# Where the first products' weights of a merge stage are loaded and split: in the merge itself, or during the stage before it

## The chip, the cores and the metric
One Trainium2 chip, the kernel on one core of it. The metric is the device time of one execution in microseconds (us), lower is better. TensorE is called PE, VectorE DVE, ScalarE ACT, GpSimd POOL; SyncE (SP) issues nearly all transfers.

## The reference, cut to what matters
One decoder layer on 2048 prompt rows and on 8 sequences of 4 new rows with 512 cached keys each. Two attention branches (differential attention a, forgetting attention b) share a projected input and are merged. The part that matters here:

```python
def _merge(x, o_a, o_b, gate_a, gate_b, m_a, m_b, gate_res, g_sub_a, w_out_a, w_out_b, w_o, lam_init):
    o_a = _rms(o_a) * g_sub_a * (1.0 - lam_init)
    y_a = (o_a.reshape(B, T, W_A) * jax.nn.silu(gate_a)) @ w_out_a
    y_b = (o_b.reshape(B, T, W_B) * jax.nn.silu(gate_b)) @ w_out_b
    y = (jax.nn.sigmoid(m_a) * y_a + jax.nn.sigmoid(m_b) * y_b) @ w_o
    return x + gate_res[:, None, :] * y
```

`w_out_a` and `w_out_b` are 512x1024, `w_o` is 1024x1024, all float32. The sample branch before it (`_sample_mix`) gathers each sequence's cached K and V pages, computes scores, softmax and the products with V. Everything is to be computed at about float32 precision.

## The kernel before
The program is a row of blocks with a barrier between them: normalise and project (two halves), maxima, attention a, attention b, **sample** (the 8 sequences' attention over the cache) and **merge** (17 tiles: 16 of 128 prompt rows, one of the 32 sample rows). Each block has one instruction stream per engine, written out by hand with semaphores; the order in the code is the order on the engine.

**Split products.** For near-float32 precision a product is made of three matmuls in a rounded format: each operand is kept as a high part (rounded) and a low part (operand less high part). `split_product` (L454) issues high x high, high x low, low x high. Weights are thus first loaded raw, then ACT copies them into the high part (L2234 in the merge), then DVE subtracts to get the low part (L2324).

**sample.** K and V pages of a sequence b (4 MB) go into one of two buffer sets by b's parity `s`; SP loads K(b) when K(b-2) has been turned and V(b) when the products with V(b-2) are done. Each turn of the loop `body(i, s)` with b = 2i+s does, besides work on sequence b, the K part of b+1: PE turns K(b+1) in eight pieces, DVE (L1900) and ACT (L1974) copy them out of PSUM, PE computes the scores of b+1, DVE adds biases and takes the maximum (L1923 to L1928), ACT the exponentials (L1984), PE multiplies probabilities of b by V. Then DVE scales and masks the result (`own_columns`, L1935) and adds it up (L1940). At the end `o_sum` is stored for the merge.

**merge.** One tile's turn: ACT squares o_a and takes sigmoids of gates (`square`, L2203, L2205) and mix (`mixing`, L2209); DVE makes u (`gated`, L2262 to L2275); PE transposes u, ACT and DVE split it (uT, L2224, L2281); PE forms both first products into ps_y (`products`, weights `w_out_a`, `w_out_b`); DVE combines them (`combine`, L2290 to L2293) into y; PE transposes y, ACT and DVE split it; PE multiplies by `w_o` into ps_o (`project_out`); DVE finishes (L2300, L2302) and SP stores. Tile n+1's u is made while tile n's products run. The first turn is written out apart, because the weights are loaded and split in it: 16 tiles of 128x1024 (kt 0 to 3 of `w_out_a`, 4 to 7 of `w_out_b`, 8 to 15 of `w_o`), through four raw buffers of which two are `x` and `out`, `w_split` counting DVE's subtractions. SP may load tile kt when `w_split` is kt-3. PE waits for `w_split` 4 and 8 before the first products and for 16 before the loop over the other tiles; SP waits for 16 before it loads x and the rows of tile 2.

Of the kernel before, what the change touches and what calls it, by code (L numbers as in the profile page):

```python
# [24 lines left out]
P = 128  # L25
# [15 lines left out]
W = 512  # L41
# [37 lines left out]
def program(nc, t):  # L79
    with ExitStack() as ctx:  # L80
# [22 lines left out]
        sample(k)  # L103
        merge(k)
# [1609 lines left out]

def sample(k):
# [10 lines left out]
    with ExitStack() as ctx:  # L1726
# [15 lines left out]
        ones = sb("ones", [NB * HB, PAST])  # L1742
        f_past = sb("f_past", [NB * HB, PAST])
# [15 lines left out]
        o_sum = sb("o_sum", [SR, 2, W])  # L1759
# [12 lines left out]
        with nc.Block() as block:  # L1772
            @block.sync
            def _(sp):
# [15 lines left out]
                def next_v(b, s):  # L1790
                    sp.wait_ge(S["made"], 1)
                    sp.wait_ge(S["pv_done"], b - 1)
                    load(b, s, 1)

                for what in range(2):
                    load(0, 0, what)
                    load(1, 1, what)
                next_k(2, 0)
                with sp.Fori(1, TURNS - 1) as i:
                    next_k(i * 2 + 1, 1)  # L1800
                    next_v(i * 2, 0)
                    next_k(i * 2 + 2, 0)
                    next_v(i * 2 + 1, 1)
                next_k(NB - 1, 1)
                next_v(NB - 2, 0)
                next_v(NB - 1, 1)
# [6 lines left out]
            def _(pool):  # L1813
# [10 lines left out]
                g.memset(ones[:], 1.0)  # L1824
# [35 lines left out]
            def _(dve):  # L1860
# [43 lines left out]
                go(v.tensor_tensor_scan(f_past[:], ones[:], ps_f, 0.0, ALU.mult, ALU.add))  # L1904
                v.tensor_scalar(f_rel[:], f_past[:], f_past[:, PAST - 1:PAST], None, ALU.subtract).then_inc(S["f_ready"], 1)
                dve.wait_ge(S["fn_ready"], 1)
                v.tensor_copy(f_new[:], ps_n[0:HB, 0:SR]).then_inc(S["fn_copied"], 1)
                go(v.memset(o_sum[:], 0.0))
# [29 lines left out]
                def add(b):  # L1938
                    dve.wait_ge(S["picked"], b + 1)
                    v.tensor_tensor(o_sum[:], ps_o[0:SR, :, :], o_sum[:], ALU.add).then_inc(S["added"], 1)  # L1940
# [4 lines left out]
                def body(i, s, first, last):  # L1945
# [14 lines left out]
                    if not last:  # L1960
                        biased(b + 1)

# [5 lines left out]
            def _(act):  # L1968
# [114 lines left out]
def merge(k):  # L2083
# [4 lines left out]
    KT = 2 * KW + KD  # L2088
    weights = [t["w_out_a"][0]] * KW + [t["w_out_b"][0]] * KW + [t["w_o"][0]] * KD
    w_row = [kt % KW if kt < 2 * KW else kt - 2 * KW for kt in range(KT)]  # L2090
    x_in = {P: t["x_prompt"][0], SR: t["x_sample"].rearrange("b t d -> (b t) d")}
    with ExitStack() as ctx:
        sb, ps, sem = tools(k, ctx, "mrg")
        w_raw = sb("w_raw", [P, 2, D])
        w = [sb("w_hi", [P, KT, D], F32R), sb("w_lo", [P, KT, D], F32R)]
# [29 lines left out]
        with nc.Block() as block:  # L2125
            @block.sync
            def _(sp):
# [20 lines left out]
                for kt in range(KT):  # L2148
                    if kt >= NW:
                        sp.wait_ge(S["w_split"], kt - NW + 1)  # L2150
                    r = w_row[kt] * P
                    sp.dma_start(w_slots[kt % NW], weights[kt][r:r + P, :]).then_inc(w_in[kt % NW], 16)
# [43 lines left out]
            def _(act):  # L2196
# [40 lines left out]
                w_high(range(2 * KW))  # L2237
                square(1, P)
                mixing(0, P)
# [194 lines left out]
```

## Time and profile before

| | us |
|---|---|
| median of 3 runs | 3129.6 (3125.41, 3134.66, 3129.6) |
| profiled execution | 3128.66 |
| its span, first to last instruction | 3127.1 |
| sample stage, first K load issued to its last store issued | 2405.68 to 2660.46 |
| merge, first transfer issued to the end | 2662.67 to 3127.1 |

The mean granted TensorE clock over the span is 0.94 of full speed. A time in the trace is counted in us from the start of the span. "Idle" is the time in which an engine had nothing before an instruction, with the instruction of another engine or the transfer that ended it.

### The profile page before, as it was taken

How to read it: one execution, taken by the hardware profiler on the slowest of the kernel's cores; microseconds unless marked ns; L12 is line 12 of the kernel's file. 1: busy time of each engine (PE TensorE's matmuls, PEld its weight loads, DVE VectorE, ACT ScalarE, POOL GpSimd, SP SyncE). 2: the span in 40 equal slices, each digit the busy share in tenths (PEclk: the TensorE clock that was granted, in tenths of full speed). 3: DMA queues.
4: the chain of work that ended last, by engine and by line, in shares of the span. 5: the costliest groups of instructions: out<-in, count | busy, mean ns of one | idle time of the engine just before them, and what ended most of it. 6: DMA issues, size and time to landing. Idle time of an engine off the chain costs nothing. (4 is left out here: it accounts for less than half of the span.)

```text
span 3127.1 us, 36974 instructions
## 1 busy us (share of the span) xinstructions
PE 2787.6 (89%) x12679; PEld 2050.4 (66%) x12679; DVE 1656.6 (53%) x2864; ACT 1040.2 (33%) x1742; POOL 196.7 (6%) x177
## 2 busy tenths in 40 slices
PE   5699999967999789999996999699997888499999
PEld 1488888855777566767774776477775322388886
DVE  2422135634265466667772776588887222545553
ACT  0411112233122256660002777555554111322221
POOL 1000002220022220000000000000001000000000
PEclk9799999987999889999997999899999899699999
DMA  5332355434453364433327562535352441533431
GB/s 209 116 101 77 101 189 156 130 123 125 148 157 104 104 134 114 117 98 95 91 76 166 133 138 62 104 82 118 74 112 77 161 149 54 202 133 124 131 127 56
DMA packets 277142, 372.85 MB, mean 119 GB/s; under 512 B 78515, under 2 KB 169779, under 8 KB 269205
## 3 DMA queue, kind: packets, MB, share of 16 engines
q1 hardware_dynamic: 275898, 370.67, 42.1%
q8 instruction: 73, 1.20, 0.2%
q14 instruction: 73, 0.60, 0.1%
q0 software_dynamic: 1056, 0.13, 0.1%
q10 hardware_dynamic: 42, 0.25, 0.0%
HBM read 259.90 MB, written 111.07 MB: 119 GB/s over the span
## 5 line engine op out<-in xcount | busy, mean ns | idle before, releaser
L454 PE MATMUL proj_z<-proj_w_hi,h_hi 128*128 128x512 f32 (+1 forms) x1200 | 475.3, 396 | 0.0
L454 PE MATMUL proj_z<-proj_w_hi,h_lo 128*128 128x512 f32 (+1 forms) x1200 | 469.8, 391 | 0.0
L454 PE MATMUL proj_z<-proj_w_lo,h_hi 128*128 128x512 f32 (+1 forms) x1200 | 468.7, 391 | 0.0
L1213 DVE TENSOR_REDUCE max_neg_top<-max_s_ps 128x1 f32<-128x1024 f32 (+7 forms) x384 | 347.1, 911 | 137.9 <-PE max_s_ps L1278 91.1
L454 PEld LDWEIGHTS proj_z<-proj_w_hi,h_lo 128*128 128x128 f32 (+1 forms) x1200 | 221.4, 185 | 53.5
L454 PEld LDWEIGHTS proj_z<-proj_w_lo,h_hi 128*128 128x128 f32 (+1 forms) x1200 | 221.9, 185 | 50.1
L454 PEld LDWEIGHTS proj_z<-proj_w_hi,h_hi 128*128 128x128 f32 (+1 forms) x1200 | 221.6, 185 | 49.7
L1624 ACT ACTIVATE att_b_pf<-att_b_s_ps,att_b_bias 128x512 f32<-128x512 f32 (+1 forms) x320 | 193.4, 624 | 160.2 <-PE att_b_s_ps L1675 80.4
L1652 DVE TENSOR_TENSOR att_b_p_lo<-att_b_pf,att_b_p_hi 128x512 fp32r<-128x512 f32 (+1 forms) x320 | 195.9, 612 | 11.0
L1177 ACT ACTIVATE max_s_ps<-max_s_ps,max_neg_top 128x128 f32<-128x128 f32 (+2 forms) x192 | 161.0, 838 | 107.0 <-DVE max_neg_top L1213 106.2
L1302 PE MATMUL max_z<-gate_w_hi,h_lo 128*128 128x512 f32 (+1 forms) x432 | 178.8, 414 | 0.0
L1302 PE MATMUL max_z<-gate_w_hi,h_hi 128*128 128x512 f32 (+1 forms) x432 | 177.9, 412 | 0.0
L1302 PE MATMUL max_z<-gate_w_lo,h_hi 128*128 128x512 f32 (+1 forms) x432 | 177.6, 411 | 0.0
L1407 ACT ACTIVATE att_a_pf<-att_a_s_ps,att_a_bias 128x1024 f32<-128x1024 f32 (+3 forms) x160 | 158.1, 988 | 53.1 <-PE att_a_s_ps L1480 32.4
L581 POOL TENSOR_TENSOR proj_rstd<-proj_rstd,keep_neg_half 128x8 f32<-128x8 f32 (+1 forms) x68 | 111.5, 1639 | 833.7 <-DVE proj_rstd L755 833.7
L1273 PE MATMUL max_s_ps<-map_k,map_q 128*128 128x512 f32 (+2 forms) x320 | 124.8, 390 | 38.4 <-ACT max_s_ps L1177 23.0
L701 DVE CAST proj_w_hi<-proj_w_raw 128x512 fp32r<-128x512 f32 x144 | 60.6, 421 | 183.9 <-PE proj_z L454 175.3
L1650 DVE CAST att_b_p_hi<-att_b_pf 128x512 fp32r<-128x512 f32 (+1 forms) x320 | 121.8, 381 | 65.6 <-ACT att_b_pf L1624 58.5
L1424 DVE SCALAR_TENSOR_TENSOR att_a_pc<-att_a_pf,keep_neg_lam 128x512 f32<-128x512 f32 (+3 forms) x160 | 106.9, 668 | 86.5 <-ACT att_a_pf L1407 86.2
L1674 PE MATMUL att_b_s_ps<-att_b_q,att_b_k 128*128 128x512 f32 (+1 forms) x320 | 121.3, 379 | 26.0 <-DMA att_b_bias<-scratch_bias_col 26.0
L683 ACT ACTIVATE proj_z_sb<-proj_z 128x512 f32<-128x512 f32 (+1 forms) x68 | 40.6, 597 | 305.7 <-PE proj_z L454 305.7
L1707 PE MATMUL att_b_acc<-att_b_p_hi,att_b_v 128*128 128x512 f32 (+1 forms) x320 | 129.6, 405 | 9.5 <-DVE att_b_p_lo L1652 9.5
(326 smaller groups left out, 5317.6 us busy)
## 6 DMA issues: line engine op xcount, KB each, us to landing
proj_w_raw<-in_w_in SPq DMA_DIRECT2D x144, 256.0 KB, 3.5
mrg_mix<-scratch_mixes SPq DMA_DIRECT2D x16, 1024.0 KB, 4.8
ada_w<-in_w_ada SPq DMA_DIRECT2D x8, 1536.0 KB, 9.1
map_qm<-scratch_q_hi SPq DMA_DIRECT2D x48, 256.0 KB
gate_w_raw<-in_w_in SPq DMA_DIRECT2D x44, 256.0 KB, 4.1
map_k<-scratch_k_hi SPq DMA_DIRECT2D x37, 256.0 KB
norm_x_in<-in_x_prompt SPq DMA_DIRECT2D x4, 2048.0 KB, 10.3
scratch_mixes<-proj_out SPq DMA_DIRECT2D x32, 256.0 KB, 2.2
```

Source lines behind the costliest of these rows:

```text
L454: ins = nc.tensor.matmul(out, left(*lt), right(*rt), start=first and n == 0, stop=last and n == len(terms) - 1)
L581: nc.gpsimd.tensor_tensor(rstd[0:pn, :], rstd[0:pn, :], k.neg_half[0:pn, :], ALU.pow).then_inc(rstd_done, 1)
L1177: nc.scalar.activation(s, s, ACT.Exp, bias=neg_top[:, kh, u, qt:qt + 1], accum_out=sums[:, kh, u, qt:qt + 1]).then_inc(sum_done, 1)
L1213: nc.vector.tensor_reduce(neg_top[:, kh, u, qt:qt + 1], s_ps[:, x % SLOTS, 0:width[x]], AX.X, ALU.max, negate=True).then_inc(max_done, 1)
L1273: nc.tensor.matmul(o, q2, k2, start=True, stop=False)
L1302: last = nc.tensor.matmul(z[0:rows_of(j), n % 2, :], h_parts[hp][:, kt, rows_j], gw.parts[wp][:, c % 2, kt, :], start=m == 0, stop=m == MM ...
L1407: nc.scalar.activation(pf[:, n % PR, :, 0:w], s_ps[:, n % PLACES, :, 0:w], ACT.Exp, bias=a.bias[h % 2][:, col:col + 1]).then_inc(p_done, 1)
L1624: nc.scalar.activation(pf[:, n % PR, 0:w], s_ps[:, n % 4, 0:w], ACT.Exp, bias=bias[s][:, kt:kt + 1]).then_inc(p_done, 1)
L1650: step.inc(nc.vector.tensor_copy(parts[HI][:, n % PR, 0:w], pf[:, n % PR, 0:w]))
L1652: nc.vector.tensor_tensor(parts[LO][:, n % PR, 0:w], pf[:, n % PR, 0:w], parts[HI][:, n % PR, 0:w].bitcast(F32), ALU.subtract).then_inc(sp ...
L1674: nc.tensor.matmul(out, k2[s][:, ks], q2[s][:, qs], start=True, stop=False)
L1707: nc.tensor.matmul(out, v[s][:, kt, 0:P], p_hi, start=kt == 0, stop=False, skip_group_check=True)
```

## The change
A new object `out_weights` holds the high and low parts of `w_out_a` and `w_out_b` and a raw buffer of two tiles, allocated around both sample and merge. In the sample stage each turn now also loads one 128x1024 tile (slot 0 from `w_out_a`, slot 1 from `w_out_b`, i the tile's number), rounds it on ACT and subtracts on DVE. The merge splits only the eight tiles of `w_o`. Its orders are rewritten for that: SP issues the first mix load ahead of weights and tile 1's rows behind the fourth weight tile, ACT does `mixing(0)` ahead of the weights, and DVE does four subtractions, `gated(1)`, two, `combine(0)`, low part, two. PE's two waits ahead of the first products go. To make room, `ones`, `f_past` and `o_sum` of the sample stage share one buffer `scan`; the memset of `o_sum` waits for `f_rel`.

```diff
+def load_out_w(k, sp, i, s):
+    w = k.out_w
+    sp.dma_start(w.raw[:, s:s + 1, :], w.src[s][:, ds(i, 1), :]).then_inc(w.loaded[s], 16)
+def out_w_high(k, act, i, s):
+    act.wait_ge(w.loaded[s], i * 16 + 16)
+    k.nc.scalar.activation(w.parts[HI][:, s:s + 1, ds(i, 1), :], w.raw[:, s:s + 1, :].unsqueeze(2), ACT.Copy).then_inc(w.hi_done[s], 1)
+def out_w_low(k, dve, i, s):
+    dve.wait_ge(w.hi_done[s], i + 1)
+    k.nc.vector.tensor_tensor(w.parts[LO][:, s:s + 1, ds(i, 1), :], w.raw[:, s:s + 1, :].unsqueeze(2),
+                              w.parts[HI][:, s:s + 1, ds(i, 1), :].bitcast(F32), ALU.subtract).then_inc(w.lo_done[s], 1)
...
+                def next_v(b, s, i):
                     sp.wait_ge(S["made"], 1)
                     sp.wait_ge(S["pv_done"], b - 1)
                     load(b, s, 1)
+                    sp.wait_ge(k.out_w.lo_done[s], i)
+                    load_out_w(k, sp, i, s)
                 for what in range(2):
                     load(0, 0, what)
                     load(1, 1, what)
+                for s in range(2):
+                    load_out_w(k, sp, 0, s)
                 next_k(2, 0)
...
                     if not last:
                         biased(b + 1)
+                    out_w_low(k, dve, i, s)
...
                     if not last:
                         k_turned(b + 1)
                         probabilities(b + 1)
+                    out_w_high(k, act, i, s)
...
                 load_o(0, P)
-                for kt in range(KT):
+                load_m(0, P)
+                for kt in range(KD):
                     if kt >= NW:
                         sp.wait_ge(S["w_split"], kt - NW + 1)
...
-                    if kt == 2 * KW - 1:
-                        load_m(0, P)
+                    if kt == NW - 1:
                         sp.wait_ge(S["u_done"], 1)
                         load_o(1, P)
-                sp.wait_ge(S["w_split"], KT)
+                sp.wait_ge(S["w_split"], KD)
                 load_x(0, P)
...
-                w_low(range(2 * KW))
+                w_low(range(4))
                 gated(1, P)
-                w_low(range(2 * KW, KT - 4))
+                w_low(range(4, KD - 2))
                 combine(0, P, True)
                 low(1, P, S["uT_hi_done"], uT, S["uT_done"])
-                w_low(range(KT - 4, KT))
+                w_low(range(KD - 2, KD))
                 low(0, P, S["yT_hi_done"], yT, S["yT_done"])
...
                     for b in range(2):
-                        if first:
-                            pe.wait_ge(S["w_split"], (b + 1) * KW)
```

On SP, at the merge's start, before (`mrg_ob`, `mrg_gates`: a tile's attention rows and gates; `mrg_w_raw`, `mrg_x`, `mrg_out`: the four raw weight buffers):

```order
L2130 DMA mrg_ob<-scratch_o_a 128x512
L2130 DMA mrg_ob<-scratch_o_b 128x512
L2131 DMA mrg_gates<-scratch_gates 128x1024
L2152 DMA mrg_w_raw<-in_w_out_a 128x1024 x2
L2152 DMA mrg_x<-in_w_out_a 128x1024
L2152 DMA mrg_out<-in_w_out_a 128x1024
L2152 DMA mrg_w_raw<-in_w_out_b 128x1024 x2
L2152 DMA mrg_x<-in_w_out_b 128x1024
L2152 DMA mrg_out<-in_w_out_b 128x1024
L2134 DMA mrg_mix<-scratch_mixes 128x2048
L2130 DMA mrg_ob<-scratch_o_a 128x512
L2130 DMA mrg_ob<-scratch_o_b 128x512
```

and after the change (`wo_raw`: the new raw buffer, now the first two of the four):

```order
L2167 DMA mrg_ob<-scratch_o_a 128x512
L2167 DMA mrg_ob<-scratch_o_b 128x512
L2168 DMA mrg_gates<-scratch_gates 128x1024
L2171 DMA mrg_mix<-scratch_mixes 128x2048
L2189 DMA wo_raw<-in_w_o 128x1024 x2
L2189 DMA mrg_x<-in_w_o 128x1024
L2189 DMA mrg_out<-in_w_o 128x1024
L2167 DMA mrg_ob<-scratch_o_a 128x512
L2167 DMA mrg_ob<-scratch_o_b 128x512
L2168 DMA mrg_gates<-scratch_gates 128x1024
L2189 DMA wo_raw<-in_w_o 128x1024 x2
L2189 DMA mrg_x<-in_w_o 128x1024
```

The eight loads of `w_out_a` and `w_out_b` are gone from here, mix stands ahead of the weights, and tile 1's rows stand behind four weight loads and not behind eight.

On DVE, from the low part of tile 0's uT to the reduction of tile 1, before:

```order
L2281 TENSOR_TENSOR mrg_uT_lo<-mrg_ps_t,mrg_uT_hi 128x512 x2
L2324 TENSOR_TENSOR mrg_w_lo<-mrg_w_raw,mrg_w_hi 128x1024 x2
L2324 TENSOR_TENSOR mrg_w_lo<-mrg_x,mrg_w_hi 128x1024
L2324 TENSOR_TENSOR mrg_w_lo<-mrg_out,mrg_w_hi 128x1024
L2324 TENSOR_TENSOR mrg_w_lo<-mrg_w_raw,mrg_w_hi 128x1024 x2
L2324 TENSOR_TENSOR mrg_w_lo<-mrg_x,mrg_w_hi 128x1024
L2324 TENSOR_TENSOR mrg_w_lo<-mrg_out,mrg_w_hi 128x1024
L2262 TENSOR_REDUCE mrg_ms<-mrg_u 128x4
```

and after, up to the combination of tile 0:

```order
L2317 TENSOR_TENSOR mrg_uT_lo<-mrg_ps_t,mrg_uT_hi 128x512 x2
L2360 TENSOR_TENSOR mrg_w_lo<-wo_raw,mrg_w_hi 128x1024 x2
L2360 TENSOR_TENSOR mrg_w_lo<-mrg_x,mrg_w_hi 128x1024
L2360 TENSOR_TENSOR mrg_w_lo<-mrg_out,mrg_w_hi 128x1024
L2298 TENSOR_REDUCE mrg_ms<-mrg_u 128x4
L2300 TENSOR_SCALAR mrg_ms<-mrg_ms 128x4
L2302 TENSOR_TENSOR mrg_gates<-mrg_gates,mrg_y 128x1024
L2304 TENSOR_TENSOR mrg_gates<-mrg_gates,mrg_gain 128x512
L2306 TENSOR_TENSOR mrg_u<-mrg_ob,mrg_gates 128x512
L2311 SCALAR_TENSOR_TENSOR mrg_u<-mrg_ob,mrg_rstd,mrg_gates 128x128 x4
L2360 TENSOR_TENSOR mrg_w_lo<-wo_raw,mrg_w_hi 128x1024 x2
L2326 TENSOR_TENSOR mrg_y<-mrg_ps_y,mrg_mix 128x1024
```

Four of the subtractions ahead of tile 1's gating are gone, and two of the four between gating and combination.

On ACT, in the sample stage, the end of a loop turn before (`smp_pr`: the exponentials):

```order
L1977 REGISTER_ALU
L1978 ACTIVATE smp_sc<-smp_ps_s 32x512
L1982 ISA
L1984 ACTIVATE smp_pr,smp_sums<-smp_sc,smp_neg_max 32x544 x2
L1853 REGISTER_ALU
L1853 COMPARE_AND_BRANCH
```

and after:

```order
L2016 REGISTER_ALU
L2017 ACTIVATE smp_sc<-smp_ps_s 32x512
L2021 ISA
L2023 ACTIVATE smp_pr,smp_sums<-smp_sc,smp_neg_max 32x544 x2
L1738 ISA
L1738 ACTIVATE wo_hi<-wo_raw 128x1024
L1890 REGISTER_ALU
L1890 COMPARE_AND_BRANCH
```

The copy into the weights' high part stands behind the exponentials, ahead of the next turn's K copies.

## Rows read from the trace of the kernel before

**Rows 1.** The page, parts 1 and 4: busy time; chain by engine.
```profile
PE 2787.6 (89%) x12679; PEld 2050.4 (66%) x12679; DVE 1656.6 (53%) x2864; ACT 1040.2 (33%) x1742; POOL 196.7 (6%) x177
...
PE 12%; DVE 1%; DMA 1%; ACT 0%; issue 0%; SPq 0%; DVEq 0%; ACTq 0%
```

**Rows 2.** Chain of waits in order, merge: start us, us, what.
```profile
2663.56 4.88 DMA mrg_ob<-scratch_o_b
...
2678.27 1.29 DVE mrg_uT_lo L2281 x2
2679.56 4.55 DVE mrg_w_lo L2324 x4
...
2686.18 8.69 DMA mrg_gates<-scratch_gates
...
2704.13 1.13 DVE mrg_y L2290
...
2707.65 1.20 DVE mrg_uT_lo L2281 x2
2708.85 3.23 DVE mrg_w_lo L2324 x3
...
2713.41 0.33 SPq L2138
...
2715.70 8.83 DMA mrg_mix<-scratch_mixes
...
2733.59 12.96 PE mrg_ps_o L454 x48
...
2747.42 11.21 PE mrg_ps_y L454 x48
```

**Rows 3.** Timeline of the merge's start: start us, us, engine, line, operation, [idle <-releaser].
```profile
2678.12 2.00 ACT L2234 ACTIVATE mrg_w_hi<-mrg_w_raw 128x1024 fp32r<-128x1024 f32 x2
...
2684.24 0.76 PE L454 MATMUL mrg_ps_y<-mrg_w_hi,mrg_uT_hi 128*128 128x512 f32 x1 [7.13 <-DVE mrg_w_lo L2324]
...
2694.26 0.69 DVE L2262 TENSOR_REDUCE mrg_ms<-mrg_u 128x4 f32<-128x512 f32 x1 [2.17 <-ACT mrg_u L2203]
...
2694.89 1.06 ACT L2205 ACTIVATE mrg_y<-mrg_gates 128x1024 f32<-128x1024 f32 x1 [0.66 <-DMA mrg_gates<-scratch_gates]
...
2695.85 1.91 ACT L2209 ACTIVATE mrg_mix<-mrg_mix 128x2048 f32<-128x2048 f32 x1
2695.98 1.23 DVE L2266 TENSOR_TENSOR mrg_gates<-mrg_gates,mrg_y 128x1024 f32<-128x1024 f32 x1 [0.83 <-ACT mrg_y L2205]
...
2697.70 0.39 PE L454 MATMUL mrg_ps_y<-mrg_w_hi,mrg_uT_lo 128*128 128x512 f32 x1
...
2699.51 2.35 DVE L2324 TENSOR_TENSOR mrg_w_lo<-mrg_w_raw,mrg_w_hi 128x1024 fp32r<-128x1024 f32 x2
...
2731.62 1.97 PE L2349 MATMUL mrg_ps_t<-keep_ident,mrg_u 128*128 128x128 f32 x8 [5.03 <-DVE mrg_u L2275]
```

**Rows 4.** Timeline of the sample stage: ACT and DVE, first turn and end.
```profile
2461.48 0.18 ACT L1984 ACTIVATION_READ_ACCUMULATOR smp_pr<-smp_sc,smp_neg_max 32x1 f32 x1
...
2466.83 1.40 DVE L1935 SCALAR_TENSOR_TENSOR smp_o_own<-smp_ps_o,smp_recip,smp_own 32x512 f32<-32x512 f32 x2 [6.86 <-PE smp_ps_o L2075]
2467.85 0.60 ACT L1974 ACTIVATE smp_kT<-smp_ps_t 128x512 f32<-128x512 f32 x1 [6.19 <-PE smp_ps_t L2013]
...
2655.43 1.40 DVE L1935 SCALAR_TENSOR_TENSOR smp_o_own<-smp_ps_o,smp_recip,smp_own 32x512 f32<-32x512 f32 x2 [11.47 <-PE smp_ps_o L2075]
```

**Rows 5.** Windows: start:end, length, busy PE, PEld, DVE, ACT, POOL; clock; DMA share, GB/s.
```profile
2440.00:2445.00 5.00, 4.29 (x20) 3.40 (x20) 1.38 (x2) 2.59 (x7) 0.00 (x0) 0.54 0.00 0
...
2668.00:2672.00 4.00, 0.00 (x0) 0.00 (x0) 1.36 (x3) 2.97 (x3) 1.04 (x1) 0.50 1.01 415
...
2684.00:2688.00 4.00, 3.76 (x9) 3.02 (x10) 1.32 (x2) 1.88 (x2) 0.00 (x0) 0.50 0.99 300
2688.00:2692.00 4.00, 4.00 (x15) 3.16 (x15) 3.58 (x3) 2.35 (x3) 0.00 (x0) 0.80 1.01 417
```

More of the change, by code:

```diff
@@ L102, in program @@
         recycle(k)
-        sample(k)
-        merge(k)
+        with ExitStack() as c4:
+            out_weights(k, c4)
+            sample(k)
+            merge(k)
 def tools(k, ctx, tag):
@@ L1712, in _, with out_weights @@
                     turn(N - 1)
+def out_weights(k, ctx):
+    nc, t = k.nc, k.t
+    _, _, sem = tools(k, ctx, "wo")
+    w = Store()
+    w.parts = [ctx.enter_context(nc.sbuf_tensor(f"wo_{n}", [P, 2, W // P, D], F32R, side="right")) for n in ("hi", "lo")]
+    w.raw = ctx.enter_context(nc.sbuf_tensor("wo_raw", [P, 2, D], F32, side="right"))
+    w.src = [t[n][0].rearrange("(a p) n -> p a n", p=P) for n in ("w_out_a", "w_out_b")]
+    w.loaded, w.hi_done, w.lo_done = [sem("loaded0"), sem("loaded1")], [sem("hi0"), sem("hi1")], [sem("lo0"), sem("lo1")]
+    k.out_w = w
+def load_out_w(k, sp, i, s):
+    w = k.out_w
+    sp.dma_start(w.raw[:, s:s + 1, :], w.src[s][:, ds(i, 1), :]).then_inc(w.loaded[s], 16)
+def out_w_high(k, act, i, s):
+    w = k.out_w
+    act.wait_ge(w.loaded[s], i * 16 + 16)
+    k.nc.scalar.activation(w.parts[HI][:, s:s + 1, ds(i, 1), :], w.raw[:, s:s + 1, :].unsqueeze(2), ACT.Copy).then_inc(w.hi_done[s], 1)
+def out_w_low(k, dve, i, s):
+    w = k.out_w
+    dve.wait_ge(w.hi_done[s], i + 1)
+    k.nc.vector.tensor_tensor(w.parts[LO][:, s:s + 1, ds(i, 1), :], w.raw[:, s:s + 1, :].unsqueeze(2),
+                              w.parts[HI][:, s:s + 1, ds(i, 1), :].bitcast(F32), ALU.subtract).then_inc(w.lo_done[s], 1)
 def sample(k):
@@ L1741, in sample @@
         tri = sb("tri", [SR, SR])
-        ones = sb("ones", [NB * HB, PAST])
-        f_past = sb("f_past", [NB * HB, PAST])
+        scan = sb("scan", [NB * HB, 2, PAST])
+        ones, f_past = scan[:, 0, :], scan[:, 1, :]
         f_rel = sb("f_rel", [NB * HB, PAST])
@@ L1758, in sample @@
         o_own = sb("o_own", [ROWS, 2, W])
-        o_sum = sb("o_sum", [SR, 2, W])
+        o_sum = scan[0:SR]
         ps_t = ps("ps_t", [P, 2, 512])
@@ L1823, in _ @@
                 g.memset(tri[:], 1.0)
-                g.memset(ones[:], 1.0)
+                g.memset(ones, 1.0)
                 g.memset(q_all[:], 0.0).then_inc(S["filled"], 1)
@@ L1903, in _ @@
                 dve.wait_ge(S["lf_turned"], 1)
-                go(v.tensor_tensor_scan(f_past[:], ones[:], ps_f, 0.0, ALU.mult, ALU.add))
-                v.tensor_scalar(f_rel[:], f_past[:], f_past[:, PAST - 1:PAST], None, ALU.subtract).then_inc(S["f_ready"], 1)
+                go(v.tensor_tensor_scan(f_past, ones, ps_f, 0.0, ALU.mult, ALU.add))
+                v.tensor_scalar(f_rel[:], f_past, f_past[:, PAST - 1:PAST], None, ALU.subtract).then_inc(S["f_ready"], 1)
                 dve.wait_ge(S["fn_ready"], 1)
                 v.tensor_copy(f_new[:], ps_n[0:HB, 0:SR]).then_inc(S["fn_copied"], 1)
-                go(v.memset(o_sum[:], 0.0))
+                dve.wait_ge(S["f_ready"], 1)
+                go(v.memset(o_sum, 0.0))
                 dve.wait_ge(S["consts"], 1)
@@ L2243, in _ @@
                 evacuate(1, P, uT[HI], S["uT_hi_done"])
-                w_high(range(KT - 4, KT))
+                w_high(range(KD - 2, KD))
                 act.wait_ge(S["y_turned"], 1)
```

33 lines of the change are left out of this document (14 added, 19 removed).

## The prediction
> **What bounds the kernel now.** First the page, its parts 1 and 4 [rows 1]. TensorE is busy 89% of the span, and the chain that ended last is 12% PE with 1% each of DVE and DMA. This chain begins with the merge's first transfer, so it says what a microsecond is worth in the merge and nothing of the sample stage; that one is read from idle times below. Second, the chain in order of time [rows 2]. From 2733.59 on it is TensorE alone, 11.21 us for 48 matmuls, turn after turn. Between 2663.56 and 2733.59 it is a start-up of 70 us in which PE is late nearly everywhere: the first attention rows (4.88), the low part of the first uT (1.29), four subtractions for the weights' low halves (4.55), the second tile's transfers (8.69), more subtractions, combine and the low part of the second tile, again four subtractions (2708.85 to 2713.41), then SP's loads for tile 2 (mix lands 8.83 us after its issue). Everything after 2733.59 only shifts with that point. So the change is worth what it takes out between 2663.56 and 2733.59, less what it adds to the sample stage.
>
> **What the change takes out of the merge.** Before, 16 weight tiles are rounded on ACT and subtracted on DVE in the merge; after, eight. I follow the chain with the durations of the trace.
> 1. Up to the low part of uT ACT and DVE have the same instructions as before. It ends at 2679.56 [rows 2].
> 2. First products. Before, they wait until DVE has subtracted four tiles: first matmul at 2684.24, with 7.13 us of idle time put down to that subtraction [rows 3]. After, both parts of these weights exist, so they start at about 2679.7. They take what they took, from 2684.24 to the last start at 2697.70 plus some 0.4: 13.85 us, of which a part is slow (the first matmul lasts 0.76; 48 of them take 11.21 in the steady part). End: 2693.5.
> 3. Is DVE ready by then? After its low part it has four subtractions, gated(1), two subtractions, combine. ACT does the sigmoid of mix (1.91) from 2678.2 and then the high parts, two in 2.00: the first is done at about 2681.2 [rows 3]. Four subtractions, 4.55: 2685.75. Meanwhile ACT ends its four high parts at 2684.2 and does tile 1's square and sigmoid (1.06), in time for the product of the gates. gated(1) took 5.25 from its reduction (2694.26) to the next subtraction (2699.51), a wait for the sigmoid included, and 4.2 without it (0.69, and 3.5 from 2695.98): 2690.0 to 2691.0. Two subtractions, 2.35: 2692.3 to 2693.4, just before the products end. So combine starts at 2693.5, where before it stood behind DVE's own queue until 2704.13.
> 4. Combine takes 3.52 (2704.13 to 2707.65), the low part of the second uT 1.20 [rows 2], then two subtractions instead of four, 2.3: 2700.55. Before, this point, from which SP may reuse the x buffer, was 2713.41. Difference 12.86, and I take 12.8.
> 5. From there the chain stays as it is: x, res, the rows of tile 2, mix with 8.83 to landing, square and gating, transposes at 2731.62, second projection at 2733.59, 20.2 us in all. PE is idle for 5.03 us before those transposes [rows 3], so the products of tile 1, which move by the same 12.8, bind nothing there.
>
> Saving in the merge: 12.8 us. Only part of it is subtractions taken away; the rest is that gated(1) moves ahead, with its loads issued once u(0) is done (before 2678.27) and not at 2686.18 behind eight weight tiles.
>
> **Transfers in the merge.** mix(0), 1 MB, is now issued right behind the first gates, ahead of the weight tiles. In the window 2668 to 2672 the transfers ran at 415 GB/s [rows 5]. The gates of tile 1 had some 3.5 MB ahead of them and landed 8.69 us after issue [rows 2], 8.4 at that rate: transfers of this queue land roughly in order. So mix behind the attention rows costs these nothing; if they shared the rate it would be 1 MB, 2.5 us. I take 0, the reading that the 8.69 is nearest to, and keep 2.5 for the range. Tile 1's rows, issued before 2678.27, land before 2683.2 with the 4.88 of the first ones, and ACT wants them at 2684.2.
>
> The Trainium skill, page "DMA: Bandwidth & Descriptors", section "Queues, rings and completion order", says that each engine takes descriptors in the order of its ring, with no promise on the order of completion across engines. By that rule the term is 0 too; the same rule is what speaks against the change in the sample stage, where two weight tiles stand ahead of K(2). The trace agrees as far as the 8.69 us go.
>
> **What it adds to the sample stage.** Eight loads of 512 KB, eight ACT copies (128x1024, 1.0 us like those removed) and eight DVE subtractions (1.2 us), one of each per sequence, behind the probabilities and behind the maximum.
> - ACT: in the first turn it idles 6.19 us between its last probability (ends 2461.66) and the next copy of K at 2467.85 [rows 4]; the later turns repeat this. 1.0 fits.
> - DVE: idle 6.86 us before its own-columns step in the first turn, 11.47 in the last [rows 4]. The subtraction waits for ACT's copy (2461.7 to 2462.7) and ends at 2463.9; own-columns begins at 2466.83. 2.9 us are left. Queued behind it are own-columns, the K copies of the next sequence and the sum, for which PE waits. With the cover gone, the whole cost is 8 x (1.0 + 1.2) = 17.6 us.
> - DMA: 4 MB beside 32 MB. In 2440 to 2445 nothing moves [rows 5], so the queue, which is full at the stage's start, is empty by 2440. The first two weight tiles put 1 MB, 2.5 us, ahead of K(2), which is then there by 2442.5; the copies of the turned K(2) start at 2467.85. The first weight tile lands before that, and ACT wants it at 2461.7. Price 0.
> - SP: one more issue per sequence, 0.33 us like the one at 2713.41. Its new wait, for the subtraction, stands behind the wait for the products with V of the same sequence; these end after that subtraction (the 2.9 us above), so it holds no K or V load queued behind it.
> - The memset of o_sum waits for f_rel two instructions ahead: 0 to 0.2 us, taken as 0.
> Sum: 0, between 0 (no work leaves this stage) and 17.6.
>
> **The sum.** The profiled execution took 3128.66 us (span 3127.1). Less 12.8: 3115.9. The median of the runs shown is 3129.6, 0.9 more; I put the forecast on the median: 3116.8, 0.41% less.
>
> **The clock term.** The granted clock is 0.50 (1.2 GHz) in 2684 to 2688, where the first matmuls run after 7.13 us of idle PE, and 0.80 in the next 4 us [rows 5]. After the change the idle time there is 4.55 shorter. Were all 48 matmuls at 2.4 GHz, they would end at 2691.3 and DVE (2692.3 to 2693.4) would bind: 0.1 to 1.2 more gained. Were all at 1.2 GHz, at most twice 11.21, they would end at 2702.1, and 8.6 of the 12.8 would be lost. I take 13.85, since it is the same burst after idle time.
>
> The Trainium skill, page "TensorE: Matmul & The Clock Gate", section "Part 1: The HAM clock gate (the "warmup" mystery)", says that the number of slow matmuls at a start differs from run to run and should not be fitted. By it this term may come out a few microseconds to either side; no run here repeats the burst yet.
>
> **Rivals.**
> - A, the forecast: 12.8 off, 3116.8. 60%.
> - B, PE runs the first products at 1.2 GHz about twice as long as before (another 2.6 us, the difference of 13.85 and 11.21) or longer, or DVE's tight 0.1 to 1.2 us in step 3 is missed by as much. For it: PE's idle times do not vanish. 6 to 10 off, about 3121. 13%.
> - C, mix delays the first attention rows: 2.5 less, 3119.3. For it: the order is a reading of one landing time. 9%.
> - D, more: higher clock in both product bursts and tighter joints, 14 to 16 off, about 3114. Against it: DVE binds step 4. 10%.
> - E, the wait is only moved: the first products start 4.55 earlier, but tile 1's chain (rows, sigmoid, gating) keeps its time, and 4.55 is all: 3125.0. Against it: its loads hang on u(0) alone. 4%.
> - F, slower: copy and subtraction lie on the sample stage's path, 17.6 against 12.8: 3134.4. It decides against the change from 1.6 us per sequence on; the rows say 6 us idle at the place. 4%.
>
> **How the numbers follow.** What a measurement of this kernel can tell from no change is about 0.3%, 9.4 us; the three runs span 3125.4 to 3134.7. Below 3120.2 lie nearly all of A and D, over half of C and a quarter of B: 0.78. Slower by as much is part of F alone, 0.03. Within: 0.19. The range: A with medians that move by 3 is 3113.5 to 3120; with D below and part of B and C above, 3111.5 to 3122.5.
>
> **What would show it.** In the profile after: the first matmul of ps_y right behind the low part of uT, its idle time released by that and by no weight subtraction, 4.5 us earlier counted from the merge's first transfer; SP's load of x and the second projection 12.8 earlier, counted likewise; combine(0) released by ps_y; the sample stage from its first K load to its store as long as before, with the new copies inside the idle times of ACT and DVE; the first rows landing after some 4.9 us. The forecast is wrong if the sample stage grows by over 1 us, if combine(0) still stands behind DVE's queue, or if tile 2's u waits for anything but mix.

## The result and the profile after

The changed kernel takes 3113.37 us (median of 5 runs, 3111.41 to 3115.26); the kernel before, 5 runs beside it, 3129.6 us. The ratio is 0.9942, 95% interval 0.9926 to 0.9958: faster by 0.42 to 0.74%. Measured a second time beside the kernel before, the ratio was 0.9953 (0.9940 to 0.9966). Forecast was 3116.8 us, range 3111.5 to 3122.5. The ratio applied to 3129.6 gives 3111.4: the sign is right, the gain was put too low (12.8 us against 16 by the medians and 18 by the ratio; the second measurement gives 17 and 15). The intervals of the whole times, 13 to 23 us and 11 to 19, do not settle the surplus by themselves; the lengths in the traces below do.

Where it is: both traces are cut at the same four points.

| us | before | after | difference |
|---|---|---|---|
| first K load to the first of the two last stores (sample) | 254.38 | 254.52 | +0.14 |
| merge's first transfer to first ps_y matmul | 21.57 | 16.80 | -4.77 |
| merge's first transfer to SP's load of x | 50.74 | 36.74 | -14.00 |
| merge's first transfer to first ps_o matmul | 70.57 | 56.42 | -14.15 |
| first ps_o matmul to that of the 16th tile | 363.28 | 357.82 | -5.46 |
| the 17th tile's ps_o, first to last start | 10.92 | 12.47 | +1.55 |
| merge's first transfer to the end | 464.36 | 446.26 | -18.10 |

The profiled executions differ by 17.25 us (3128.66 and 3111.41), since the work ahead of the merge took 0.8 longer in the second one. Over all profiles this part wandered by 11 us (first K load at 2398.5 to 2409.3), so what follows compares lengths counted from the merge's first transfer.

The page after, parts 1 and 4, stands to [rows 1] like this:

```profile
PE 2784.6 (90%) x12679; PEld 2051.1 (66%) x12679; DVE 1657.6 (53%) x2864; ACT 1040.4 (33%) x1742; POOL 197.9 (6%) x177
...
PE 13%; DVE 1%; DMA 0%; ACT 0%; issue 0%; SPq 0%; ACTq 0%; DVEq 0%
```

The instruction counts are the same: work was moved, none removed. PE is busy 3.0 us less, with the same 12679 matmuls. So the same matmuls became shorter on the whole; whether by the clock or by something else this line does not tell.

The chain of waits in order, the merge after the change (start us, us, what), answers to [rows 2]:

```profile
2664.40 4.74 DMA mrg_ob<-scratch_o_b
...
2678.97 1.30 DVE mrg_uT_lo L2317 x2
...
2680.31 12.74 PE mrg_ps_y L456 x48
...
2696.76 1.20 DVE mrg_uT_lo L2317 x2
2697.96 2.28 DVE mrg_w_lo L2360 x2
...
2700.25 0.33 SPq L2175
...
2702.55 8.67 DMA mrg_mix<-scratch_mixes
...
2720.28 11.65 PE mrg_ps_o L456 x48
...
2732.80 10.92 PE mrg_ps_y L456 x48
...
2744.59 11.21 PE mrg_ps_o L456 x48
...
3092.09 12.88 PE mrg_ps_o L456 x48
```

Four subtractions (4.55) and the second tile's transfers (8.69) are gone from the chain, and the whole first product stands there in their place. Look at the lines at 2732.80 and 2744.59 as well. Before, every 48 matmuls of the steady part took 11.21, ps_y [rows 2] and ps_o alike; one of the latter in the chain of before:

```profile
2759.51 11.20 PE mrg_ps_o L454 x48
```

Now those of ps_o still do, and those of ps_y take 10.92. Nothing in the change touches the steady part of the merge but the place of the weights.

The timeline of the merge's start after the change answers to [rows 3]:

```profile
2680.31 0.79 PE L456 MATMUL mrg_ps_y<-wo_hi,mrg_uT_hi 128*128 128x512 f32 x1 [2.50 <-DVE mrg_uT_lo L2317]
...
2684.93 1.05 ACT L2241 ACTIVATE mrg_y<-mrg_gates 128x1024 f32<-128x1024 f32 x1
...
2690.56 2.35 DVE L2360 TENSOR_TENSOR mrg_w_lo<-wo_raw,mrg_w_hi 128x1024 fp32r<-128x1024 f32 x2
...
2693.14 1.23 DVE L2326 TENSOR_TENSOR mrg_y<-mrg_ps_y,mrg_mix 128x1024 f32<-128x1024 f32 x1 [0.23 <-PE mrg_ps_y L456]
```

The first matmul waits for the low part of uT alone. DVE ends its sixth subtraction at 2692.91, and combine begins 0.23 later, released by PE.

The sample stage after (to [rows 4]):

```profile
2462.40 1.04 ACT L1738 ACTIVATE wo_hi<-wo_raw 128x1024 fp32r<-128x1024 f32 x1
2463.47 1.23 DVE L1744 TENSOR_TENSOR wo_lo<-wo_raw,wo_hi 128x1024 fp32r<-128x1024 f32 x1 [2.67 <-ACT wo_hi L1738]
2467.66 1.40 DVE L1973 SCALAR_TENSOR_TENSOR smp_o_own<-smp_ps_o,smp_recip,smp_own 32x512 f32<-32x512 f32 x2 [2.96 <-PE smp_ps_o L2115]
2468.68 0.60 ACT L2013 ACTIVATE smp_kT<-smp_ps_t 128x512 f32<-128x512 f32 x1 [5.24 <-PE smp_ps_t L2053]
```

Copy and subtraction lie inside the two idle times: of DVE's 6.86 are left 2.96 behind the subtraction, of ACT's 6.19 are left 5.24. PE still releases both instructions.

The granted clock at the first products (windows; columns as in [rows 5]):

```profile
2680.00:2684.00 4.00, 3.69 (x10) 2.92 (x11) 2.54 (x4) 4.00 (x5) 0.00 (x0) 0.55 0.11 27
2684.00:2688.00 4.00, 4.00 (x19) 3.30 (x18) 3.97 (x6) 3.04 (x4) 0.78 (x1) 1.00 0.82 264
```

The burst begins at 1.2 GHz as before, and is at 2.4 GHz in the next four microseconds, where before the second window had 0.80.

### The profile page after: what moved, and what is told of

Same layout as the page of the kernel before. It is cut to its first block and busy times, and to the rows that moved or that the text cites. A ratio compares the mean times of both kernels' runs of the same rounds, so it can differ in the third digit from the quotient of the medians.

```text
span 3109.8 us, 36991 instructions
## 1 busy us (share of the span) xinstructions
PE 2784.6 (90%) x12679; PEld 2051.1 (66%) x12679; DVE 1657.6 (53%) x2864; ACT 1040.4 (33%) x1742; POOL 197.9 (6%) x177
```

## The experiments

Two questions. First, the forecast's mechanism took 14 us out of the start-up: which part of the change did that, and does the work moved into the sample stage really cost nothing? Second, something else took 4 to 5 us out of the steady part: what? The suspect for the second is where the buffers begin. In these products the transposed rows (uT, yT) are the stationary operand, 128x128, that PE loads ahead of each matmul, and the kernel's weights are the moving operand, 512 columns at a time; "operand" below, without more, is uT or yT. The program places both one behind the other in each partition's memory, and the change shifts them: modulo 256 bytes, the weights began at 160 before and uT and yT at 224. After the change the weights of ps_y lie at the other end of the memory and begin at 224, like uT, and those of ps_o still at 160. The rival is that ps_y gained from something else: two separate weight tensors, DMA traffic, or the earlier start.

### Offsets: four kernels measured side by side

`e1_swap_offsets`: the change, with 192 unused bytes ahead of `u`.

```diff
+        sb("gap", [P, 48])
         u = sb("u", [P, 2 * W])
```

> The changed kernel with one gap of 192 bytes per partition in the merge's buffers, so that the transposed operands (uT, yT) begin at byte 160 modulo 256 instead of 224. The weights wo stay at 224, those of w_o at 160. Theory O (a matmul is faster, 227 ns a step against 233, when its weights buffer and its transposed operand lie at the same offset modulo 256): the two products swap, steady ps_y 48 matmuls in 11.2 us, ps_o in 10.9, and the whole time as the changed kernel's, 3113, within 1. Theory A (it is the absolute offset or the place of the weights, right end of the memory, that makes them fast): ps_y stays at 10.9, ps_o at 11.2. Theory N (the gain in ps_y is due to other engines' work beside it): nothing moves, 10.9 and 11.2.

Measured: 3106.79 us (4 runs), ratio 0.9932 (0.9915 to 0.9948). In the steady part 48 matmuls of ps_o (offsets now equal, at 160) and of ps_y (weights 64 above the operand) take, in the chain in order:

```profile
2742.47 10.90 PE mrg_ps_o L456 x48
2754.25 10.99 PE mrg_ps_y L456 x48
```

ps_o, which the change had left at 11.21, has the short time, as theory O said. But ps_y, 64 above, nearly keeps it where 11.2 was expected, so unequal starts are not slow as such, and the whole time is 3106.79 and not the 3113 expected.

`e2_wo_and_w_near`: the change, with 64 bytes ahead of the `w_o` weights and 192 behind them, so all begin at 224.

```diff
+        sb("gap1", [P, 16])
         w = [sb("w_hi", [P, KD, D], F32R), sb("w_lo", [P, KD, D], F32R)]
+        sb("gap2", [P, 48])
```

> The changed kernel with gaps of 64 and 192 bytes around the w_o weights, so that these too begin at 224 modulo 256, like uT, yT and wo. Theory O: ps_o also takes 10.9 us a tile, 16 tiles by 0.3: 4.8 us less than the changed kernel, about 3108.5. Theory of place (right end): ps_o unchanged at 11.2 and 3113.

Measured: 3106.08 us (4 runs), ratio 0.9929 (0.9912 to 0.9945). Both products take 10.9 for 48 matmuls; the merge is 443.55 us long, 2.7 less than with the change alone and not the 4.8 less expected: the steady part gave 4.0, but the first ps_o burst took 12.68 between first and last start instead of 11.60, by its clock.

`e3_before_shifted`: the kernel before with the same two gaps; nothing of the change.

> The kernel before with the same gaps: all merge weights at 224 modulo 256 like uT and yT, no other edit. Theory O: both products 10.9 instead of 11.2 a tile, 33 by 0.3, 9 to 10 us less than before: 3120. Place or other engines: 3129.6, nothing.

Measured: 3123.08 us (10 runs, spread widely, 3115.07 to 3127.36), ratio 0.9981 (0.9972 to 0.9991): 6 us less by whole times (3 to 9), where 9 to 10 were expected. The profile is of the fastest of the ten, so it is read for lengths. The merge is 453.85 us long, 10.5 less than before: 28 steady products by 0.29 are 8.1, and 1.6 are the first ps_o burst (12.92 before, 11.28 here), most of it its clock (9 and 2 steps of 427 ns); the rest lies at the merge's start and end. Chain in order:

```profile
2765.84 10.92 PE mrg_ps_y L454 x48
2777.64 10.90 PE mrg_ps_o L454 x48
```

This is the clearest of them: not one instruction is different from the kernel before but for the addresses, and every steady product of 128 rows is 0.3 us shorter.

`e4_before_all_moved`: the kernel before with only the first gap. Weights at 224, operands at 32: another place, the same distance (64 below).

> The kernel before with one gap of 64 bytes ahead of the weights, which moves weights and transposed operands alike: weights at 224, uT and yT at 32 modulo 256, same difference as before. Theory O (only the difference matters): 11.2 a tile in both products. If the weights' own offset of 224 is what counts: 10.9.

Measured: 3128.77 us (one run). Chain in order, the products as slow as before:

```profile
2771.89 11.20 PE mrg_ps_y L454 x48
2783.97 11.19 PE mrg_ps_o L454 x48
```

So it is the distance between the two operands, not the place of the weights at 224. The distance counts modulo 256: 10.9 came where weights and operand lie an odd multiple of 256 bytes apart (ps_y of the change, 196576 and 122592) and where it is an even one (`e2_wo_and_w_near`, 196576 and 122848).

The trace of the kernel before has such a pair too, in a stage that no experiment touched. In the first projecting stage the same `split_product` has weights and stationary operand both at 160. Windows of that stage, its matmuls alone (start:end, length, busy PE, PEld, DVE, ACT; clock; DMA share, GB/s):

```profile
201.00:401.00 200.00, 200.00 (x884) 165.68 (x883) 0.00 (x0) 22.64 (x38) 1.00 0.29 92
```

That is 226 to 227 ns for each of 884 matmuls of the form that took 233.5 in the merge. In the second projecting stage both buffers begin at 160 as well, but a row of the stationary one is 4224 bytes long, so every other 128x128 tile begins 128 bytes further on, and a step takes some 232 ns in the mean; the lengths found below for 0 and 128 would give 230. The start of a buffer is thus not enough to tell the time; no run varied the tiles' starts one by one.

### The change with the old distance, and its other parts

`c0_change_again` is the changed kernel once more, measured beside the three that follow.

> The changed kernel itself, for comparison with the others of this call. 3113, or 16 below before; ps_y 10.9, ps_o 11.2 a tile.

Measured: 3112.98 us (6 runs), ratio 0.9953 (0.9940 to 0.9966). Its profile repeats the first to about 0.1 us: sample stage 254.45, load of x 36.63, first ps_o 56.33, first to 16th tile 357.84, merge 446.17.

`e5_old_offsets`: the change with 64 bytes ahead of the `w_o` weights (weights at 224, operands at 32).

```diff
+        sb("gap1", [P, 16])
         w = [sb("w_hi", [P, KD, D], F32R), sb("w_lo", [P, KD, D], F32R)]
```

> The changed kernel with one gap of 64 bytes ahead of the w_o weights: both products then have the offsets of before (weights 64 bytes below the transposed operand, modulo 256). So only what the prediction spoke of is left of the change. Theory O: ps_y back to 11.2 a tile, 4.5 us more than the changed kernel, and against before the 12.8 us of the prediction, plus or minus the clock of the start-up bursts. Rival (the surplus is not the offsets but the clock or the start-up): same time as the changed kernel.

Measured: 3115.18 us (5 runs), ratio 0.9954 (0.9942 to 0.9967). Chain in order, its start-up and first steady products:

```profile
2680.20 12.81 PE mrg_ps_y L456 x48
2720.31 12.97 PE mrg_ps_o L456 x48
2734.15 11.20 PE mrg_ps_y L456 x48
```

Load of x 37.14 and first ps_o 56.89 after the merge's first transfer, first to 16th tile 363.05 (before: 363.28), merge 450.39. This is the change as the forecast had it: 13.97 us off the merge, against 12.8. By whole times the step is not resolved: the medians are 2.2 us apart, but the ratios of the two kernels are alike and each is uncertain by 4 us. It rests on the lengths in the traces, 363.05 against 357.82 and 357.84.

`e6_late_rows`: the change, with the first mix and tile 1's rows behind all eight weight loads on SP, and ACT in the order that fits.

```diff
                 load_o(0, P)
-                load_m(0, P)
                 for kt in range(KD):
...
-                    if kt == NW - 1:
+                    if kt == KD - 1:
+                        load_m(0, P)
                         sp.wait_ge(S["u_done"], 1)
                         load_o(1, P)
...
-                mixing(0, P)
                 w_high(range(4))
                 square(1, P)
+                mixing(0, P)
```

> The changed kernel, but mix(0) and tile 1's rows are loaded behind all eight w_o tiles, and ACT does mixing(0) behind tile 1's square, as in the kernel before. If most of the 12.8 us is due to gated(1) moving ahead, the loads of tile 1 are issued at about 2688 (behind the eighth tile) and land at about 2695, gating ends near 2701, and the point from which SP loads x comes 9 us later: 9 us slower than the changed kernel. If it is due to the eight tiles fewer to split, the same time as the changed kernel within 2.

Measured: 3122.24 us (7 runs), ratio 0.9973 (0.9962 to 0.9984). SP's load of x comes 45.99 us after the merge's first transfer, 9.25 later than with the change; the first matmul of ps_y is where it was (16.85). The merge is 454.32 us long, 8.1 more than with the change (446.17), and the medians are 9.3 apart. The profile is of the fastest of the seven (3112.76 us), and its sample stage, whose code is the same, took 255.66: a length of this stage can move by 1.2 us by itself. The chain in order, from the issue of tile 1's attention rows on:

```profile
2679.49 0.71 SPq L2167
...
2680.24 8.55 DMA mrg_gates<-scratch_gates
2688.81 1.06 ACT mrg_y L2241
...
2694.56 1.22 DVE mrg_w_lo L2360
2695.78 1.13 DVE mrg_y L2326
...
2700.50 2.27 DVE mrg_w_lo L2360 x2
...
2702.79 0.33 SPq L2175
```

The 8.69 of tile 1's transfers in [rows 2] are back (8.55). So of the 14 us, 9.25 go with the place of these loads in SP's queue (and the order on ACT that fits it). The other 4.75 are read from this chain: from the landing of tile 1's gates to combine(0) 6.99 (9.26 before), and behind the low part 2.29 until SP's load of x (4.56 before). These are the four subtractions fewer in DVE's queue behind tile 1's gating, two ahead of combine and two behind it. The first products start 4.8 earlier here too and bind nothing. The two parts do not simply add up, though. In the changed kernel combine waits for the first products; had these started as late as before (21.57) and taken their 12.74, combine would have come some 4.8 later (an estimate from the two traces). So the 9.25 need both: the loads early and no subtraction ahead of the first products.

`e7_copies_twice`: the change, and in each turn of the sample stage one ACT copy and one DVE subtraction more of the same size. The additional ones write a fixed place and are not used.

```diff
+    for j in range(1):
+        ...
+        k.nc.scalar.activation(w.parts[HI][:, s, W // P - 1, :], w.raw[:, s, :], ACT.Copy).then_inc(w.again[0], 1)
...
+    for j in range(1):
+        ...
+        k.nc.vector.tensor_tensor(w.parts[LO][:, s, W // P - 1, :], w.raw[:, s, :], w.parts[HI][:, s, 0, :].bitcast(F32), ALU.subtract).then_inc(w.again[1], 1)
```

> The changed kernel with an extra ACT copy and an extra DVE subtraction of the same size beside each of the eight in the sample stage. DVE had 2.96 us of idle time left in a turn: copies end 1.05 later, subtractions 2.3 later, 0.7 left. Theory: the sample stage as long as before, 254.4 us from first K load to the first store. Rival F (they lie on the path): 8 times 2.2, 272.

Measured: 3114.21 us (one run), sample stage 254.34 us, no longer than with one pair. Timeline of the first turn:

```profile
2468.59 1.22 DVE L1758 TENSOR_TENSOR wo_lo<-wo_raw,wo_hi 128x1024 fp32r<-128x1024 f32 x1
...
2470.43 1.40 DVE L1987 SCALAR_TENSOR_TENSOR smp_o_own<-smp_ps_o,smp_recip,smp_own 32x512 f32<-32x512 f32 x2 [0.61 <-PE smp_ps_o L2129]
```

The idle time of DVE ahead of its own-columns step shrinks from 2.96 to 0.61, and PE still ends it. Rival F would have given 272.

### How far the cover reaches, other distances, and one step further

`e8_copies_four`: the same with four pairs a turn.

```diff
-    for j in range(1):
+    for j in range(3):
```

> The change, with the rounding and the subtraction of each of the eight tiles in the sample stage done four times instead of once (the extra ones into a fixed place, their results unused). Done twice they cost nothing: the sample stage took 254.34 us against 254.52. Theory (the cover is finite, and is what the idle times of DVE and ACT there show): ACT gets 4.2 us of work before a stretch in which it was idle 5.24 us; DVE's subtractions end about 3.9 us after the point (2467.66) from which its own columns could start. So each of seven turns is some 3.9 us late, up to 27 us for the stage, less what the later steps of a turn take up; between 8 and 27 us longer, and the end as much later. Rival (DVE's idle time there is not what bounds a turn): the stage stays at 254.5 and the end within 3 us of 3113.

Measured: 3148.07 us (one run), sample stage 293.22, that is 38.7 longer, beyond the 27 that the theory allowed. Timeline of the first turn, DVE's last subtraction and what is queued behind it, and PE's transposes:

```profile
2468.75 1.23 DVE L1758 TENSOR_TENSOR wo_lo<-wo_raw,wo_hi 128x1024 fp32r<-128x1024 f32 x1
2469.89 1.39 DVE L1987 SCALAR_TENSOR_TENSOR smp_o_own<-smp_ps_o,smp_recip,smp_own 32x512 f32<-32x512 f32 x2
...
2471.94 1.97 PE L2067 MATMUL smp_ps_t<-keep_ident,smp_k_a 128*128 128x128 f32 x8 [5.06 <-DVE smp_kT L1951]
```

Counted from the bias sum of the same turn (2461.38 with one additional pair, 2456.85 here), own-columns begins 13.0 us after it instead of 9.05: 4.0 late, the 3.9 of the theory. What it left out comes behind: the K copies queued on DVE make it 5.4 by the start of the next scores. PE has meanwhile waited 5.06, and the granted clock falls (windows):

```profile
2480.00:2490.00 10.00, 8.83 (x18) 2.04 (x18) 1.55 (x7) 0.00 (x0) 0.00 (x0) 0.83 0.63 210
```

In the changed kernel it is 1.00 at this place. The scores take 8.33 instead of 7.03, and the turn is 6.75 longer in this case, 5.5 in the mean of seven. So a late step costs more than its lateness: of the 6.75, 4.0 are DVE's subtractions, 1.4 the K copies queued behind them and 1.3 PE's clock. The clock's part differs by turn; in two of the last six turns the scores of the changed kernel are as slow (18 matmuls take 9.1 us between first and last start, 7.4 in the other four), so the first turn's 1.3 are not a price for every turn.

`e10_other_offsets`: the change with gaps of 224 and 160 bytes. Weights of ps_y lie 128 above their operand, those of ps_o 32 above.

```diff
+        sb("gap1", [P, 56])
         w = [sb("w_hi", [P, KD, D], F32R), sb("w_lo", [P, KD, D], F32R)]
+        sb("gap2", [P, 40])
```

> The change with two unused gaps in the memory, of 224 and 160 bytes per partition: modulo 256 the loaded weights now begin at 128, the ones ahead at 224, and both transposed operands at 96. So for the products of ps_y the weights lie 128 above the operand, for those of ps_o 32 above. Seen so far: 0 gives 227.5 ns a step, 64 above 229.2, 64 below 233.3. Theory (only the distance of the two starts counts, and it is the lower start of the weights that costs): ps_o at 32 above between 227.5 and 229.2, ps_y at 128 (above and below are the same there) between 227.5 and 233.3. Rival (the step depends on the operand's own place, or on whether the two are equal): ps_o at 233, as every unequal pair but one gave. Nothing else moves: x load 36.7 us after the merge's first transfer; the end between 3104 and 3114.

Measured: 3114.98 us (one run), merge 451.1. Chain in order:

```profile
2757.29 11.15 PE mrg_ps_y L456 x48
2769.31 11.21 PE mrg_ps_o L456 x48
```

The whole time is 1 us above the expected stretch. My rule (only weights below cost) is false: 32 above costs as much as 64 below. The rival, that only equal starts are quick, is contradicted by 64 above in `e1_swap_offsets`; that the operand's own place also counts is not excluded, since +32, +64 and 128 were each seen at one place only. Measured so far, for 48 matmuls, weights' start less the operand's, modulo 256: 0 gives 10.90 to 10.93, +64 gives 10.99 to 11.01, 128 gives 11.15, +32 and -64 give 11.19 to 11.21. What rule makes these is open.

`e11_rows_ahead`: `e2_wo_and_w_near`, and SP issues tile 2's attention rows and its mix as soon as their buffers are free.

```diff
+                sp.wait_ge(S["u_done"], 2)
+                load_o(2, P)
+                sp.wait_ge(S["y_done"], 1)
+                load_m(1, P)
                 sp.wait_ge(S["w_split"], KD)
                 load_x(0, P)
...
-                turn(0, P, P, first=True)
                 with sp.Fori(1, TILES - 2) as n:
```

> The change with equal offsets (3106.08 us in its run), and one more edit: SP issues the attention rows and the mix rows of tile 2 as soon as their buffers are free, ahead of its wait for the last subtraction of the loaded weights and of x and res, instead of behind them. Theory (the second projection waits for the mix rows of tile 2, which land 8.7 us after an issue that stands behind x): issued some 5 us earlier they land earlier, the second projection starts about 4.5 us earlier, and the end is at about 3101.5; then the first output products of PE are the next bound. Rival (the transfers share bandwidth with the last weight tiles, and the wait only moves from mix to the weights): within 1 us of the kernel with equal offsets in the same call.

Measured: 3101.84 us (4 runs), ratio 0.9907 (0.9890 to 0.9923), the lowest median of all. Against `e12_near_again`, measured beside it, that is 3.9 us less, and the intervals of the two ratios overlap; the traces tell more. The merge is 6.6 shorter (433.55 against 440.15), and the first ps_o begins 50.45 us after its first transfer, 5.9 earlier. Chain in order, from the last subtractions on:

```profile
2699.11 2.28 DVE mrg_w_lo L2365 x2
2701.39 0.33 issue
2701.72 12.81 PE mrg_ps_y L456 x48
2714.53 0.87 PE mrg_ps_t L2390 x8
2715.41 10.93 PE mrg_ps_o L456 x48
```

The mix is gone from the chain, as expected. PE's products are now the bound from 2701.72 on; what is left ahead of them is PE's wait for the eighth subtraction, behind which stand tile 1's first products.

`e12_near_again` is `e2_wo_and_w_near` once more, measured beside it.

> The change with equal offsets, once more, beside the kernel that has one edit more. Theory (the step is 227.5 ns in both products): 3106 us, as the first time, ratio to the kernel before 0.992 to 0.993, merge stage 443.5 us. Rival (the gain of 7 us was this kernel's place on one chip): 3110 to 3113.

Measured: 3105.75 us (4 runs), ratio 0.9922 (0.9905 to 0.9938), like the 0.9929 of its first run, on another chip. The change alone gave 0.9942 and 0.9953; it was never measured beside this kernel, and the intervals overlap in part. What is sure are the lengths in the traces: from the first ps_o to the 16th tile's 354.93 and 353.61 us, with the change alone 357.82 and 357.84. The merge is 440.15 us long, 3.4 less than in its first run: same program, another number of matmuls at 1.2 GHz. The chain in order, first and last ps_o, of its first run:

```profile
2717.55 12.72 PE mrg_ps_o L456 x48
...
3086.17 12.87 PE mrg_ps_o L456 x48
```

and of this one:

```profile
2719.13 11.40 PE mrg_ps_o L456 x48
...
3086.43 11.32 PE mrg_ps_o L456 x48
```

Two bursts after idle time, 1.3 and 1.6 us apart between executions of one program.

## Why the forecast was right in sign and too small

**The step that failed** is the sentence "Everything after 2733.59 only shifts with that point", with its 11.21 per product. It rested on the steady rows of before and on the fact that the code of the loop is not changed. But an instruction whose text is the same reads its weights from another place. Between the first and the 16th tile's ps_o 5.46 us went: 1.3 are the first ps_o burst (12.92 before, 11.60 after, between first and last start), and some 4.1 the steady part, where fourteen products of ps_y by 0.29 make 4.1 (the fifteenth, of the 32 sample rows, took 10.97 and 10.96). The swap (`e1_swap_offsets`), the old distance restored (`e5_old_offsets`) and the kernel before with gaps alone (`e3_before_shifted`) show that the distance of the two operands' starts does it. The rival causes fall with the last one: it has none of the change. The term belonged into the sum with -4.1 and was not there at all. The merge's rows of before could not show it, since both products stood at the same distance there; the first projecting stage of the same trace could have (227 ns a step against 233.5), and the forecast did not look there.

**Step 1** (same work up to the low part of uT): right, 15.46 us from the merge's first transfer, 15.60 before.

**Step 2** (start 4.55 earlier, burst unchanged at 13.85): start 4.77 earlier. The burst took 12.74, so this term was mis-sized by 1.1. Its clock: before, 11 matmuls behind the first start 427 ns apart, with the change 5 to 7 in every profile but that of `e8_copies_four`, where there were again 11. A few microseconds either way was the text's bound; the runs show 1.1. That each of three profiles without the change has 11 or more, and ten of the eleven with it 5 to 7, speaks against luck alone; but the burst of `e8_copies_four` begins where that of the change does (16.68 us from the merge's first transfer) and has 11, so what sets the count is open.

The Trainium skill, page "TensorE: Matmul & The Clock Gate", section "Part 1: The HAM clock gate (the "warmup" mystery)", warns that the count of slow matmuls differs from run to run. The trace agrees for the first and last ps_o: the two runs of one program with equal offsets have 11.40 and 12.72, 11.32 and 12.87. For the first ps_y it hardly differed between executions of the change (6 in both profiles).

**Step 3** (DVE just ready): right in order, with 0.23 us to spare. That this lies within the 0.1 to 1.2 is luck: the burst was 1.1 shorter than there, and DVE was ready at 29.40 us from the merge's first transfer where 29.6 to 30.7 were put. **Step 4** (x load 12.86 earlier): 14.00, the 12.86 and the 1.1 of step 2; combine, low part and two subtractions took 3.62, 1.20 and 2.28 where 3.52, 1.20 and 2.3 were put. **Step 5** (the chain behind it unchanged): right, 19.68 from the load of x to the first ps_o against 19.83.

**The place of the loads** (9 of the 14 us): that gating moved ahead is most of the gain stands in the forecast, and `e6_late_rows` gives 9.25 of it back.

**The clock term** has a slip that nothing hangs on: 48 matmuls at 2.4 GHz from 2679.7 on end at 2690.9, not 2691.3.

**Transfers**: mix ahead of the weights cost nothing. The first rows landed in 4.74 us with mix and four weight tiles issued behind them, 4.88 before. Rival C (2.5 us) is out. The reading beneath the term was loose. 3.5 MB is what SP had issued ahead of tile 1's gates since 2680.72; at the 140 and 300 GB/s of the windows from 2680 and 2684 on, about 1.2 MB of it had moved by 2686.18. That the 3.5 MB gave the 8.4 is chance; that the first loads land first is what both kernels show.

**Sample stage at nothing**: right, +0.14. `e7_copies_twice` shows the slack, `e8_copies_four` its end. Rival F, slower, named the right place: one of the three additional pairs is covered (`e7_copies_twice`), the other two would cost 16 x 2.2 = 35.2 by its formula, and 38.7 were lost. That the two are near is partly luck, since the formula holds neither the queue behind DVE nor the clock.

**Rivals B and E** are out: the 4.77 of the first start are followed by 14.00 at the load of x. **Rival D** (more, about 3114, by clock and tighter joints) came nearest to the time and is half right: the clock gave 1.1 and 1.3, and took 1.55 back at the last product, so 0.9 in all. The 4.1 that made the difference were in no case of the text, and so not in its range either.

## What to carry to other kernels

Where a change moves buffers, the instructions that it leaves alone are no longer sure to keep their time: list the starts of the operands that PE reads, before and after, and look at one steady product of each kind, in the other stages too: one form with two lengths in one trace is the sign. A gain that a trace shows where the diff shows nothing is found fastest by putting the buffers of the old kernel where the new ones are, with nothing else changed. And at a stage's start ask first which loads stand in the queue behind others that are needed later: here they went with nearly twice what the subtractions taken out of DVE's queue gave (9.25 us against 4.75), and again 5.9 us when tile 2's rows were drawn ahead.

## What the runs showed of the hardware

- A steady product of 48 matmuls (stationary operand 128x128, moving operand 512 columns, rounded format) at 2.4 GHz took 10.90 to 11.21 us, 227.1 to 233.5 ns a matmul, by the start of the moving operand (here the kernel's weights) less that of the stationary one (the transposed rows), modulo 256 bytes: shortest at 0, 10.99 to 11.01 at +64, 11.15 at 128, 11.19 to 11.21 at +32 and -64. The place of both together made no difference where it was varied, at 0 and at -64 (weights and operand both at 160 or both at 224; 64 apart at 160 and 224 or at 224 and 32). Other distances were not measured, and whether it is the load of the stationary operand or the read of the moving one that waits is open.
- After 5.06 us of idle PE the granted clock was 0.83 over the next stretch of the sample stage, and sixteen matmuls took 8.33 instead of 7.03 us (`e8_copies_four`).
